# Expert weights in 2 MB units with 16 KB in one run per partition, in place of 1 MB units

## What is computed

```python
logits = hf @ router_w + router_b;  top_vals, top_idx = lax.top_k(logits, 4);  gates = softmax(top_vals)
def run_block(tok, e):                      # tokens of expert e
    gu = xb @ w_gate_up[e] + b_gate_up[e]   # w_gate_up (32, 1024, 2048)
    gate = minimum(gu[:, :1024], 7.0);  up = clip(gu[:, 1024:], -7.0, 7.0)
    act = gate * sigmoid(1.702 * gate) * (up + 1.0)
    return act @ w_down[e] + b_down[e]      # w_down (32, 1024, 1024)
```

## Time and profile before

| | us |
|---|---|
| median of three runs | 1166.28 |
| the profiled execution, its time | 1164.85 |
| the profiled execution, its span | 1163.0 |
| TensorE busy | 1052.1 |
| VectorE busy | 301.9 |
| ScalarE busy | 147.0 |

### The profile page before, as it was taken

The page is one execution under the profiler, slowest core; times in us unless marked ns, Lnnn a source line. Parts: engine busy times, 40 slices in busy tenths (PEclk is TensorE's granted clock), DMA queues, the critical chain, the costliest instruction groups (busy, mean ns, idle before and its releaser), DMA issues.

```text
span 1163.0 us, 12236 instructions
## 1 busy us (share of the span) xinstructions
PE 1052.1 (90%) x4662; PEld 432.9 (37%) x4662; DVE 301.9 (26%) x594; ACT 147.0 (13%) x239; POOL 5.2 (0%) x12
## 2 busy tenths in 40 slices
PE   7999999889898989999999898989898989898987
PEld 4444544533434343434343333233333333332323
DVE  2554122231313131313122213131313131222212
ACT  3124101110101010101011101010101010101010
POOL 1000000000000000000000000000000000000000
PEclk9999999799999999999999999999999999999999
DMA  9933234799999999999999999999999999999996
GB/s 350 369 132 124 77 145 141 301 386 384 417 420 414 422 415 422 414 422 415 423 414 422 415 421 414 423 414 422 416 422 415 422 416 419 417 420 418 417 420 257
DMA packets 84018, 430.36 MB, mean 370 GB/s; under 512 B 7952, under 2 KB 8080, under 8 KB 51232
## 3 DMA queue, kind: packets, MB, share of 16 engines
q1 hardware_dynamic: 83168, 428.12, 90.8%
q0 software_dynamic: 544, 1.90, 0.5%
q10 hardware_dynamic: 288, 0.08, 0.0%
HBM read 429.03 MB, written 1.05 MB: 370 GB/s over the span
## 4 chain that ended last, share of the span: by engine, by line
SPq 47%; PE 43%; issue 4%; DVE 2%; DMA 2%; ACT 1%; DVEq 0%; PEldq 0%
SPq L258 47%; PE bank L1048 15%; PE bank L835 9%; PE bank L1105 7%; PE bank L862 5%; PE bank L1010 2%; PE bank L1120 2%; DMA hT<-w_down_dram 2%; PE bank L810 1%; DVE big L767 1%; PE bank L1017 1%; PE bank L983 0%; DMA consts<-consts_dram 0%; DVE big L785 0%; PE bank L1023 0%
## 5 line engine op out<-in xcount | busy, mean ns | idle before, releaser
L1048 PE MATMUL bank<-ring,big 128*64 128x512 f32 x1536 | 346.1, 597 | 14.1 <-DMA ring<-w_gate_up_dram 7.5
L1048 PEld LDWEIGHTS bank<-ring,big 128*64 128x64 f32 x1536 | 105.2, 136 | 239.2 <-issue 199.3
L1105 PE MATMUL bank<-ring,big 128*64 128x512 f32 x768 | 169.2, 595 | 4.9 <-DMA ring<-w_down_dram 4.9
L835 PE MATMUL bank<-ring,hT 128*128 128x512 f32 (+1 forms) x256 | 103.4, 562 | 1.4 <-DVE hT L469 0.8
L760 DVE COPY big<-bank 128x512 f32<-128x512 f32 x32 | 22.1, 692 | 316.6 <-PEq L1068 177.7
L1105 PEld LDWEIGHTS bank<-ring,big 128*64 128x64 f32 x768 | 54.3, 137 | 107.6 <-issue 105.2
L1010 PE MATMUL bank<-kqT,xn 128*128 128x128 f32 x544 | 68.4, 287 | 19.9 <-DVE big L767 19.0
L1120 PE MATMUL bank<-big,kqT 128*128 128x512 f32 x128 | 61.8, 615 | 15.1 <-DVE big L785 15.1
L1010 PEld LDWEIGHTS bank<-kqT,xn 128*128 128x128 f32 x544 | 65.7, 201 | 23.4 <-DVE big L767 22.3
L431 ACT ACTIVATE big<-bank 128x512 f32<-128x512 f32 x32 | 19.1, 598 | 413.9 <-PEq L1068 262.2
L785 DVE COPY big<-bank 128x512 f32<-128x512 f32 x16 | 11.1, 692 | 223.9 <-PEq L1110 223.9
(11 more groups left out here) (214 smaller groups left out, 675.8 us busy)
## 6 DMA issues: line engine op xcount, KB each, us to landing
ring<-w_gate_up_dram SPq DMA_DIRECT2D x192, 1024.0 KB, 20.6
ring<-w_down_dram SPq DMA_DIRECT2D x96, 1024.0 KB, 20.9
siga<-w_gate_up_dram SPq DMA_DIRECT2D x16, 1024.0 KB, 21.8
sigp<-w_gate_up_dram SPq DMA_DIRECT2D x16, 1024.0 KB, 23.0
qo<-w_gate_up_dram SPq DMA_DIRECT2D x16, 1024.0 KB, 24.4
hT<-w_gate_up_dram SPq DMA_DIRECT2D x16, 1024.0 KB, 26.3
ring<-w_in_dram SPq DMA_DIRECT2D x14, 1024.0 KB, 15.6
siga<-w_down_dram SPq DMA_DIRECT2D x8, 1024.0 KB, 20.7
```

Source lines behind the costliest of these rows:

```text
L835: ins = MM(bank[PAIR_BANKS[j % 3][b]][:, 0:n], hT[:, kc, b * P:b * P + P], w[:, k, :], start=kc == 0, stop=kc == KC - 1)
L1048: ins = MM(bank[2 * e + h][T * g:T * g + T, :], xgT[:, k, T * e:T * e + T], ring[s][:, D * g + 512 * h:D * g + 512 * h + 512], start=k == ...
L1105: ins = MM(bank[4 + h][T * e:T * e + T, :], actT[:, c, T * e:T * e + T], v3(ring[ws[e]][:, :], 2)[:, k, 512 * h:512 * h + 512], start=c == ...
```

## The change

A unit is now 2 MB. A gate/up unit is 256 rows of `w_gate_up`, partition p holding rows 2p and 2p + 1 (16 KB that lie together in memory). A down unit is 512 rows, partition p holding 4p to 4p + 3 (16 KB again). The ring has 8 slots of 2 MB: six `ring` tiles, `sgates` (the old `siga` and `sigp`) and `hq` (the old `hT` and `qo`). The first part keeps its 1 MB units, in the halves of the six tiles.

```diff
-RING = 12
-EXTRA = 4
+RING = 6
+EXTRA = 2
+HALVES = 2 * RING
-UW = 2048
+UW = 4096
...
-                row = (2 * p + u // 8) * D + (u % 8) * P
-                return w_gu[bass.ds(row, P), :]
-            row = (2 * p + j % 2) * D + (j // 2) * 2 * P
-            return w_dn[bass.ds(row, 2 * P), :].rearrange("(k p) n -> p k n", p=P)
+                row = (2 * p + u // 4) * D + (u % 4) * 2 * P
+                return w_gu[bass.ds(row, 2 * P), :].rearrange("(p k) n -> p (k n)", k=2)
+            row = (2 * p + j % 2) * D + (j // 2) * 4 * P
+            return w_dn[bass.ds(row, 4 * P), :].rearrange("(p k) n -> p (k n)", k=4)
```

```diff
-MM(TB[h][:, k * P:k * P + P], xn[:, b, c * P:c * P + P], ...
+MM(TB[h][:, k * P:k * P + P], xn[:, b, c // 2 * 2 * P + c % 2:c // 2 * 2 * P + c % 2 + 2 * P - 1:2], ...
-nc.tensor.transpose(TB[h][:, k * P:k * P + P], src[:, c * P:c * P + P], ident)
+c0 = c // rows * rows * P + c % rows        # rows = 4
+nc.tensor.transpose(TB[h][:, k * P:k * P + P], src[:, c0:c0 + rows * (P - 1) + 1:rows], ident)
```

A slot is released after two chunks of gate/up, and in the down loop after four chunks on two slots:

```diff
-                    ins.then_inc(unit_used[s], 1)
+                    if k % 2 == 1:
+                        ins.then_inc(slot_used[s], 1)
...
-                for k2 in range(KC // 2):
+                for k2 in range(KC // 4):
-                                if k == 1 and h == 1:
-                                    ins.then_inc(unit_used[ws[e]], 1)
+                                if k == 3 and h == 1:
+                                    ins.then_inc(slot_used[ws[e]], 1)
```

The host lays `bgu` and the norm gain out as before, so TensorE and VectorE turn them once into the new order, after `projection(0)`:

```diff
+            def turn_tables():
+                pe.wait_ge(bgu_in, 16)
+                pe.wait_ge(cols_in, 16)
+                for k in range(4):
+                    for g in range(4):
+                        MM(bank[4][32 * g:32 * g + 32, k * P:k * P + P], ident[:, k::4],
+                           bgu_t[:, :].rearrange("p (e j c g) -> p e j c g", e=E, j=2, c=4)[:, :, :, g, :],
+                           start=True, stop=True)
+                for k in range(2):
+                    for g in range(2):
+                        ins = MM(bank[5][64 * g:64 * g + 64, 4 * k:4 * k + 4], ident[:, k::2], cols[:, P_G2 + g:P_G2 + g + 7:2],
+                                 start=True, stop=True)
+                ins.then_inc(turned_ready, 1)
+                pe.wait_ge(turned_read, 2)
...
             projection(0, lambda: turn_x(1))
+            turn_tables()
...
+            dve.wait_ge(turned_ready, 1)
+            V.tensor_copy(bgu_t[:, :]..., bank[4][:, :]...).then_inc(turned_read, 1)
+            V.tensor_copy(g2_t[:, :]..., bank[5][:, 0:KC]...).then_inc(turned_read, 1)
+            dve.wait_ge(turned_read, 2)
```

More of the change, by code:

```diff
@@ L110, in block_kernel @@
         rank_t = sb("rank", NB * E)
+        g2_t = sb("g2", KC)
         gat_t = sb("gates", NB * E)
-        ring += [siga_t, sigp_t, qo_t, hT_t]
+        half = [ring[s // 2][:, HW * (s % 2):HW * (s % 2) + HW] for s in range(HALVES)]
+        ring += [sg_t, hq_t]
         ident = consts[:, K_IDENT:K_IDENT + P]
@@ L161, in block_kernel @@
         TB = [bank[6], bank[7]]
-        unit_in = [sem(f"unit_in{s}") for s in range(SLOTS)]
-        unit_used = [sem(f"unit_used{s}") for s in range(SLOTS)]
+        unit_in = [sem(f"unit_in{s}") for s in range(HALVES)]
+        unit_used = [sem(f"unit_used{s}") for s in range(HALVES)]
+        slot_in = [sem(f"slot_in{s}") for s in range(SLOTS)]
+        slot_used = [sem(f"slot_used{s}") for s in range(SLOTS)]
+        bgu_in, turned_ready, turned_read = sem("bgu_in"), sem("turned_ready"), sem("turned_read")
         x_in = [sem("x_in0"), sem("x_in1")]
@@ L240, in _ @@
             sp.dma_start(x[:, 0, :], x_d[0:P, :]).then_inc(x_in[0], 16)
-            for s in range(RING, SLOTS):
-                sp.sem_inc(unit_in[s], 16 * PRE_TURNS)
             def pre_unit(u):
-                s = u % RING
-                if u >= RING:
-                    sp.wait_ge(unit_used[s], u // RING)
+                s = u % HALVES
+                if u >= HALVES:
+                    sp.wait_ge(unit_used[s], u // HALVES)
                 src, w = pre_unit_src(u)
                 k = 4 if u < 16 else 2
-                sp.dma_start(v3(ring[s][:, 0:w], k), src).then_inc(unit_in[s], 16)
+                sp.dma_start(v3(half[s][:, 0:w], k), src).then_inc(unit_in[s], 16)
             def pair_unit(p, v):
                 s, u = v % SLOTS, v % PAIR_UNITS
-                dst = ring[s][:, :] if u < 16 else v3(ring[s][:, :], 2)
                 src = pair_unit_src(p if v < PAIR_UNITS else p + 1, u)
-                sp.dma_start(dst, src).then_inc(unit_in[s], 16)
+                sp.dma_start(ring[s][:, :], src).then_inc(slot_in[s], 16)
             pre_unit(0)
@@ L278, in next_turn @@
             def next_turn(p, turns, t):
-                used = sp.snap(turns + (t + PRE_TURNS))
+                used = sp.snap(turns + (t + LEAD))
                 for s in range(SLOTS):
-                    sp.wait_ge(unit_used[s], used)
+                    sp.wait_ge(slot_used[s], used)
                     pair_unit(p, (SLOTS * t + s) % (2 * PAIR_UNITS))
@@ L794, in _ @@
             MM = nc.tensor.matmul
-            for s in range(RING, SLOTS):
-                pe.sem_inc(unit_used[s], PRE_TURNS)
+            for s in range(SLOTS):
+                pe.sem_inc(slot_used[s], LEAD)
             tj = [0]
@@ L813, in unit @@
             def unit(u):
-                s = u % RING
-                pe.wait_ge(unit_in[s], 16 * (u // RING + 1))
-                return ring[s]
+                s = u % HALVES
+                pe.wait_ge(unit_in[s], 16 * (u // HALVES + 1))
+                return half[s]
             def free_unit(u, ins):
-                ins.then_inc(unit_used[u % RING], 1)
+                ins.then_inc(unit_used[u % HALVES], 1)
             def free_banks(j):
@@ L1040, in all_used @@
                     t, s = divmod(PAIR_UNITS * half + u, SLOTS)
-                    pe.wait_ge(unit_used[s], turns[t])
+                    pe.wait_ge(slot_used[s], turns[t])
                 def gate_up(e, k):
-                    s = landed(8 * e + k)
+                    s = landed(4 * e + k // 2)
                     for h in range(2):
                         for g in range(2):
+                            c0 = HW * (k % 2) + D * g + 512 * h
                             ins = MM(bank[2 * e + h][T * g:T * g + T, :], xgT[:, k, T * e:T * e + T],
-                                     ring[s][:, D * g + 512 * h:D * g + 512 * h + 512], start=k == 0, stop=k == KC - 1)
-                    ins.then_inc(unit_used[s], 1)
+                                     ring[s][:, c0:c0 + 512], start=k == 0, stop=k == KC - 1)
+                    if k % 2 == 1:
+                        ins.then_inc(slot_used[s], 1)
                 for h in range(2):
@@ L1087, in pair_step @@
                     pe.wait_ge(gu_copied[1][h], c2)
[L1088 removed]
+                    turn("TB", gu_sb, h, 4)
                 for h in range(2):
@@ L1124, in two_pairs @@
             def two_pairs(count, it, with_bias):
-                turns = [count(3 * it + (t + 1 + PRE_TURNS)) for t in range(3)]
-                turns_in = [count(48 * it + 16 * (t + 1 + PRE_TURNS)) for t in range(3)]
+                turns = [count(3 * it + (t + 1 + LEAD)) for t in range(3)]
+                turns_in = [count(48 * it + 16 * (t + 1)) for t in range(3)]
                 for half in range(2):
```

63 lines of the change are left out of this document (33 added, 30 removed).

## The result

1156.26 us as the median of four runs (1155.8 to 1156.7), beside 1166.35 for the kernel before in the same comparison: a ratio of 0.991, with an interval of 0.9895 to 0.9926. The profiled execution took 1156.41 us with a span of 1154.6. Between the profiled executions the change is 8.4 us, between the medians 10.1, since the profiled execution of the kernel before lay 1.5 under its median and this one 0.15 over its own.

A forecast was written before the change was run, and what follows sets the result against it. The weight stream was taken as the bound from the second pair on; -21.0 (stream) + 3.4 (restart) + 3.4 (tail) + 5.3 (tables) = -8.9 us gave 1156.0 profiled, 1157.4 as median, range 1152 to 1174.

The forecast's parts named there:

- (a): Expert weight stream, restart to last landing: 352 MB at 2.45 us per MB, 865.0 us after 886.0, gain 21.0.
- the line: DMA rate by packet size: about 2.415 us per MB plus 9 ns per packet, so 428 GB/s at 16 KB.
- Rival 1: Stream: no better than 8 KB runs, 1170.4 us (cut at 4 KB, 1193.7); 0.25 with rates on the way, 0.07 for cut or slowdown.
- (b): Restart after the first pair's issue hole: slot released after 32 down-loop instructions, not 16, +3.4 us.
- Rival 3: Ring too coarse: longer TensorE stops open stream holes; 2 us in each of the first two pairs gives 1161; chance 0.05.
- (c): Tail at the kernel's end: 32 instructions after the last landing, not 16, +3.4 us.
- (d): Tables turned between the first two projections: twenty small matmuls plus a wait for VectorE's copies, +5.3 us.
- (e): SyncE's fewer waits and issues, and qo's prefetch later by 8 us: no cost.
- (f): Gather and transposes reading with a step in each pair: no cost on the path, at most 3.4 us a pair.
- Its sign: Profile sign for free stepped reads: groups of 8 transposes at 1.04 to 1.09 us, gather at 3.8.
- rival 2: Stepped reads in turn and gather make TensorE the bound from 1.2 us a pair; 0.13 for beyond 1.75.
- Its room: TensorE's spare time behind the stream's end: 19.2 us over about 16 pairs, 1.2 us a pair.

The follow-up runs named there:

- e5: Changed kernel with each 2 MB unit fetched in two 1 MB transfers, one 8 KB run per partition each; 1169.74 us, ratio 1.0023.
- e6: Changed kernel with each 2 MB unit fetched in two 1 MB transfers, two 4 KB runs per partition each; 1198.25 us, ratio 1.0269.
- e2: Changed kernel with TensorE's wait for VectorE's two table copies moved behind projection(1); 1157.65 us, ratio 0.991, in two groups of times.
- e7: Changed kernel with each transpose of both turns done three times, result unchanged; 1198.66 us, ratio 1.0272.
- e9: Changed kernel with ScalarE's and VectorE's copies writing the new column order, so TensorE reads neighbours again; 1162.85 us, ratio 0.9958.
- e1: Changed kernel's 2 MB units and ring, but the earlier row layout (8 KB runs, 4 KB for down), no stepped reads or tables; 1177.13 us, ratio 1.0087.
- e4: Changed kernel with the eight transposes of the second turn (TB) done twice in every pair, result unchanged; 1157.74 us, ratio 0.9918.
- e12: Changed kernel with the table matmuls moved behind the first router rank, where TensorE was idle; 1150.08 us, ratio 0.9862, in two groups of times.

## Why the prediction was right

The time, 1156.26, lies 1.1 below the forecast 1157.4. That difference is chance: on the profiled executions the forecast was -8.9 and the change -8.4, 0.5 the other way, and what is left is how far each profiled execution lay from its median. By its steps:

(a) **Stream.** The forecast was 865.0 us from restart to last landing, and 865.8 were measured. The rate beyond the rows of before, 428 GB/s, came as the line said; e5 and e6 show the line on one program, with 879.3 us at 8 KB (878.0 by the line) and 907.0 at 4 KB (901.3). Rival 1 is refuted: with 8 KB runs the time is 1169.74 (forecast for this rival 1170.4), with 4 KB 1198.25 (1193.7).

(b) **Restart.** The later release cost 3.5 us (forecast 3.4), the hole 14.3 (about 14). It opens once, in the first pair: every slice of the page from the eleventh to the last but one is at 426 GB/s or more. Rival 3 did not occur.

(c) **Tail.** +3.5 (forecast 3.4).

(d) **Tables.** The forecast was 5.3; the chain was late by 5.6 behind `projection(2)` and by 4.9 at the first down loop. The sum is right by luck, since two errors cancel. The sixteen matmuls of 32 columns were costed like the gather's 32 instructions, 3.8 us, and took 1.19. They go to four different 32-column groups of the array, and follow each other at about 37 ns where the gather's have 120. Together with the four small ones and the wait they put `projection(1)` back by 2.4 us and not by 5.3. In their place came a cost without a term: the granted clock fell to 1.2 GHz for 6.8 us, and the two projections there took (5.54 - 3.77) + (15.42 - 13.99) = 3.2 us more. In e2, without the wait, they took 3.79 and 13.97; but in e6 and e7 they were as short with the wait, so what makes the clock fall is open.

(e) No cost seen: with a restart and a stream as forecast, nothing is left for it.

(f) **Stepped reads.** The forecast took no cost on the path. Its sign for that, groups of 8 transposes at 1.04 to 1.09 us and a gather of 3.8, did not come. The mean of a weight load, from the groups of before and after:

```profile
L1010 PEld LDWEIGHTS bank<-kqT,xn 128*128 128x128 f32 x544 | 65.7, 201 | 23.4 <-DVE big L767 22.3 <-issue 1.1
...
L1017 PEld LDWEIGHTS bank<-consts,big 128*128 128x128 f32 x256 | 27.4, 140 | 40.7 <-issue 40.7
```

```profile
L1035 PEld LDWEIGHTS bank<-kqT,xn 128*128 128x128 f32 x544 | 75.5, 223 | 21.9 <-DVE big L776 20.8 <-issue 1.1
...
L1043 PEld LDWEIGHTS bank<-consts,big 128*128 128x128 f32 x256 | 33.3, 210 | 40.7 <-issue 40.7
```

A load of the transpose, read 16 bytes apart, went from 140 to 210 ns, and a turn from 1.06 (as in e9, which reads without a step) to 1.21 us; the gather, read 8 bytes apart, from 3.81 to 4.01. The mean load of the gather is no measure of its step: it is 233 ns in e9, which reads without a step, as it includes loads at the lower clock. A pair grew by 0.4 us, far from rival 2's 1.2. The Trainium skill ("SBUF — State Buffer", the note on cachelines of 16 bytes) wants two hits in a line; the trace agrees in the direction for the transposes, at 0.15 us a turn, not at the 1.4 us a pair that the prediction tied to it. The gather pays a little too, which the rule does not give.

What the forecast left out is the clock in the pairs, and so it came nearer to rival 2 than it says. Its room, 19.2 us over the pairs, is 20.3 when worked out with the measured starts (281.21 + 15 x 56.4 + 7.1 = 1134.3 against 1154.6). The step used 15 x 0.4 = 6.0 of it. Another 8.5 went to the granted clock, which fell to 1.2 GHz for 3.4 us in the second turn or the gather of six of the sixteen pairs, 1.4 us each time; it had done so in one pair before. Some 1.2 us are spread over the rest. One of the falls:

```profile
318.10:321.50 3.40, 2.39 (x11) 2.42 (x12) 3.06 (x6) 0.63 (x1) 0.00 (x0) 0.63 1.04 443
```

This is the stretch of the gather of 5.48 us above. The 4.6 us that were left are the 4.6 us of waits for data on the page. So the step was free as forecast, by a margin a quarter as wide as reckoned. The one wait of some 2 us that the forecast expected in a pair came in the last three pairs only, since TensorE starts the pairs a full ring behind (before the change its waits began at 644.85 us) and the step and the falls lengthen its pairs. The slower loads don't explain the falls: e1, with the old loads, had eleven of them, and e4, with more transposes, none. By what the pairs that have one are picked stays open, and so do the two groups of times in e2 and e12.

## What to carry to other kernels

Where a stream of weights bounds a kernel, read its rate per packet size: if the sizes already in the trace lie on one line, the next larger run can be forecast from it, and the run that a partition gets counts, not the size of the transfer. Put against it what the coarser unit costs in its three places (slot released later, longer work behind the last landing, data in another order), since here they took back 12 of 20 us, and place the reordering where its engine is idle anyway, which lowered the median by 6.2 us here (three of five executions by 6.2 to 7.0, two by 1.1 to 1.4). When a stretch differs between kernels, look whether the clock fell in it before giving the time to the edit. When the freed stream comes within some 2 us a period of the next engine, count that engine's short pauses and clock falls as well, and not its busy time alone.

## What the runs showed of the hardware

- The rate of the expert stream on one core by packet was 409 to 413 GB/s at 4 KB, 421 to 422 at 8 KB and 428 to 430 at 16 KB. At 4 and 8 KB transfers of 1 and 2 MB differed by 1% at most. It fits about 9 ns per packet of a DMA engine on top of 2.41 us per MB.
- 32 instructions that use 32 columns each, spread over the four column groups, took 1.19 us; 32 that use all 128 columns took 3.81.
- A wait of 0.87 us on TensorE, behind small matmuls, was followed by about 6.8 us at 1.2 GHz and 3.2 us of loss in the profiles of four kernels (the change, e4, e5, e9), and by no fall in those of two (e6, e7). In e2, without the wait, there was none at that place, but one came later, at 97.8 us.
- A ScalarE copy of 128 x 512 from a bank took 597 ns, and 1268 when elements that are neighbours in the bank were written 512 bytes apart; on VectorE it was 692 and 1256.
- A weight load of 128 x 128 float32 read 16 bytes apart took 210 ns (140 when contiguous). Eight such transposes took 1.20 to 1.23 us (1.06 to 1.09), and a gather of 32 instructions whose loads read 8 bytes apart 4.01 us (3.81).
